# First projections of a two-layer decoder step: where ScalarE loads its sigmoid table, in which order the first block's gates and weight parts are made, and how many result tiles are split beside the last block's gates

## The reference

```python
proj = u @ w_in                            # u = rms_norm(x), w_in 2048 x 5120
xr, gate = proj[..., :D_RNN], proj[..., D_RNN:]          # D_RNN = 2560
xc = conv_b + sum(xpad[:, k:k + T] * conv_w[k] for k in range(4))
xb = xc.reshape(B, T, N_LRU_BLOCKS, LRU_BLOCK)           # 10 blocks of 256
r = sigmoid(einsum('btnc,ncd->btnd', xb, w_r) + b_r)
i = sigmoid(einsum('btnc,ncd->btnd', xb, w_i) + b_i)
log_a = -8 * r * softplus(-lam);  a = exp(log_a)
b = sqrt(-expm1(2 * log_a)) * (i * xc)
h_t = a_t * h_{t-1} + b_t                                # a scan over the tokens
y = (h * silu(gate)) @ w_out                             # w_out 2560 x 2048
```

## Time and profile before

| | |
|---|---|
| median of 3 executions | 1761.04 us (1760.8 to 1763.99) |
| the profiled execution | 1762.91 us, span 1761.2 us |
| PE busy | 1699.5 us (96% of the span), 13907 matmuls |
| DVE busy | 1151.5 us (65%) |
| ACT busy | 973.4 us (55%) |
| POOL busy | 235.6 us (13%) |

### The profile page before, as it was taken

How to read it: one execution, slowest core, us unless ns; L and a number is a source line. 1 busy time by engine, 2 the same in 40 slices (tenths; PEclk the granted TensorE clock), 3 DMA queues, 4 the chain that set the end, 5 groups by cost and what they waited for, 6 DMA issues and landing times.

```text
span 1761.2 us, 34973 instructions
## 1 busy us (share of the span) xinstructions
PE 1699.5 (96%) x13907; PEld 1645.7 (93%) x13907; DVE 1151.5 (65%) x1921; ACT 973.4 (55%) x1643; POOL 235.6 (13%) x182
## 2 busy tenths in 40 slices
PE   7989999999999999999999999999999999899996
PEld 7889999999999999999999999999998999899995
DVE  5878888888889522468767566665666666722365
ACT  6656665566566422355566666666675666522344
POOL 2000000000000010103232222222321111011110
PEclk9999999999999999999999999999999999999998
DMA  8423333233235233664622222222225787423565
GB/s 278 130 85 105 101 109 109 85 113 104 89 113 180 72 93 89 189 178 126 195 85 61 73 73 60 85 60 61 85 61 151 233 249 234 142 84 87 153 179 179
DMA packets 317096, 217.63 MB, mean 124 GB/s; under 512 B 9265, under 2 KB 287937, under 8 KB 316865
## 3 DMA queue, kind: packets, MB, share of 16 engines
q1 hardware_dynamic: 309724, 197.08, 38.1%
q10 hardware_dynamic: 4356, 9.32, 1.4%
q0 software_dynamic: 2864, 9.15, 1.4%
HBM read 195.10 MB, written 20.42 MB: 122 GB/s over the span
## 4 chain that ended last, share of the span: by engine, by line
PE 41%; DVE 5%; issue 2%; ACT 1%; DMA 1%; SPq 1%; ACTq 0%; DVEq 0%
PE PS L858 11%; PE PS L859 10%; PE PS L860 10%; PE Z L1279 2%; DVE T L2638 1%; PE Z L1289 1%; PE Z L1313 1%; PE Z L1185 1%; PE Z L1216 1%; DVE Y L2885 1%; PE Z L1182 1%; PE Z L1194 1%; PE Z L1183 1%; PE Z L1218 1%; PE Z L1217 1%
## 5 line engine op out<-in xcount | busy, mean ns | idle before, releaser
L858 PE MATMUL PS<-U,WS 128*128 128x272 f32 x2528 | 747.0, 295 | 12.9 <-DVE WS L2202 2.7
L860 PE MATMUL PS<-U,WS 128*128 128x272 f32 x2528 | 732.6, 290 | 0.0
L859 PE MATMUL PS<-U,WS 128*128 128x272 f32 x2528 | 730.9, 289 | 0.0
L858 PEld LDWEIGHTS PS<-U,WS 128*128 128x128 f32 x2528 | 478.4, 189 | 19.6 <-issue 9.2
L859 PEld LDWEIGHTS PS<-U,WS 128*128 128x128 f32 x2528 | 478.1, 189 | 2.0
L860 PEld LDWEIGHTS PS<-U,WS 128*128 128x128 f32 x2528 | 477.5, 189 | 0.0
L2177 DVE TENSOR_TENSOR WS<-raw,WS 128x1024 fp32r<-128x1024 f32 (+1 forms) x184 | 231.7, 1260 | 192.3 <-ACT WS L1492 190.8
L1492 ACT ACTIVATE WS<-raw 128x1024 fp32r<-128x1024 f32 (+1 forms) x186 | 192.3, 1034 | 249.5 <-PE PS L860 229.6
L736 POOL TENSOR_TENSOR raw<-raw,GN 128x1024 f32<-128x1024 f32 x76 | 151.0, 1987 | 517.6 <-DMA raw<-in_b_w_in_dram 443.4
L973 PE MATMUL PS<-U,WS 128*128 128x272 f32 x432 | 125.2, 290 | 0.0
L975 PE MATMUL PS<-U,WS 128*128 128x272 f32 x432 | 125.0, 289 | 0.0
(11 more groups left out here) (384 smaller groups left out, 3587.3 us busy)
## 6 DMA issues: line engine op xcount, KB each, us to landing
raw<-in_a_w_in_dram SPq DMA_DIRECT2D x80, 512.0 KB, 3.8
raw<-in_b_w_in_dram SPq DMA_DIRECT2D x64, 512.0 KB, 4.1
raw<-in_a_w_out_dram SPq DMA_DIRECT2D x32, 512.0 KB, 3.9
KPG<-in_cache_k_dram SPq DMA_DIRECT2D x64, 256.0 KB, 3.1
raw<-in_b_w_out_dram SPq DMA_DIRECT2D x32, 512.0 KB, 3.9
VPG<-in_cache_v_dram SPq DMA_DIRECT2D x60, 256.0 KB, 3.3
T<-scratch_x SPq DMA_DIRECT2D x64, 136.0 KB, 3.3
RAW<-in_a_w_out_dram SPq DMA_DIRECT2D x12, 512.0 KB, 4.0
```

The costliest lines, as they stand in the source:

```text
L858: pe.matmul(psum, w_hi, x_hi, start=first, stop=False)
L859: pe.matmul(psum, w_hi, x_lo, start=False, stop=False)
L860: return pe.matmul(psum, w_lo, x_hi, start=False, stop=last)
```

## The change

There is a new one-column tile `WARM`, and `sigmoid_table()` writes a Sigmoid of one column into it, so that the table load stands at that place. It is called in block 0 ahead of the gates, and in every later block in `two_strips(i, 1)` after `keep(p, 2)`. In block 0 the difference 0 and unit 8's high part come earlier, the gate sigmoids come ahead of the two SiLU sigmoids, and DVE follows that order. In block 9 output unit 1's weights and the tiles 8 and 9 are split between the gate sigmoids, the tiles 10 and 11 and output unit 2's weights ahead of `chain_square` (on DVE ahead of `one_minus_a2`, which now precedes the tiles 12 to 15).

```diff
--- before.py
+++ after.py
@@ -206,6 +206,7 @@
+        WARM, _ = sb("WARM", [P, 1])
@@ -1676,6 +1677,9 @@
                     T[:, 4 + 2 * g + o, 0:TOK].rearrange("p (a n) -> p a n", a=2), gate_bank(n, i)[:, :, 0:HALF],
                     ACT.Sigmoid, bias=CH[:, 2 * i + o, ROW_BR + g:ROW_BR + g + 1]).then_inc(gates_out, 1)
 
+            def sigmoid_table():
+                nc.scalar.activation(WARM[:], GN[:, 0, 0:1], ACT.Sigmoid)
+
             def first_block():
                 gate_high(0)
                 conv_tap(0, 0)
@@ -1688,22 +1692,23 @@
                     x_scaled(kt)
                 high(7, 1, 3)
                 conv_high(0, 1)
+                act.wait_ge(unit_done, 7)
+                difference_high(0, U[:, 0:KQ, half(1)])
                 difference_high(1, XT[:, 0, 0])
+                high(8, 0, 4)
                 difference_high(2, XT[:, 2, 0])
                 difference_high(3, XT[:, 1, 0])
-                act.wait_ge(unit_done, 7)
-                difference_high(0, U[:, 0:KQ, half(1)])
-                high(8, 0, 4)
-                sigmoid_gate(0, 0)
+                sigmoid_table()
+                second_half(8)
                 gate_sigmoid(0, 0)
-                second_half(8)
                 gate_sigmoid(0, 1)
-                sigmoid_gate(0, 1)
                 first_sum(8, 0)
                 gate_sigmoid(0, 2)
+                gate_sigmoid(0, 3)
                 second_sum(0)
+                sigmoid_gate(0, 0)
+                sigmoid_gate(0, 1)
                 third_sum(0)
-                gate_sigmoid(0, 3)
 
             def two_strips(i, q, last):
 
@@ -1743,6 +1748,8 @@
                 act.wait_ge(s_done, 3 * p + 2)
                 act.wait_ge(strip_out, 4 * i + 2 * q)
                 keep(p, 2)
+                if q:
+                    sigmoid_table()
                 if last and q:
                     y_back(3)
                 if q == 0:
@@ -1761,16 +1768,19 @@
                 if last:
                     for kt in range(1, 5):
                         y_split(kt)
+                    act.wait_ge(y_done, i * 2)
                     sigmoid_gate(i, 0)
                     y_split(5)
-                    act.wait_ge(y_done, i * 2)
                     gate_sigmoid(i, 0)
                     y_split(6)
                     gate_sigmoid(i, 1)
+                    high(B0 + 1, 1, (B0 + 1) // 2, done=A_UNITS)
                     y_split(7)
                     gate_sigmoid(i, 2)
+                    y_split(8)
                     sigmoid_gate(i, 1)
                     gate_sigmoid(i, 3)
+                    y_split(9)
                     return
                 m, p = pair(i + 1, 0)
                 second_half(m)
@@ -1789,12 +1799,12 @@
             first_block()
             for i in range(1, NBLK):
                 block_a(i, i == NBLK - 1)
-            high(B0 + 1, 1, (B0 + 1) // 2, done=A_UNITS)
-            y_split(8)
-            y_split(9)
             chain_decay(NBLK - 1)
+            y_split(10)
+            y_split(11)
+            high(B0 + 2, 0, (B0 + 2) // 2)
             chain_square(NBLK - 1)
-            for kt in range(2 + UT, KD):
+            for kt in range(12, KD):
                 y_split(kt)
 
             def square(n, par, src):
@@ -1806,7 +1816,7 @@
             def pair_b(i, first):
                 for n in range(6):
 
-                    if not (first and n == 0):
+                    if not (first and n <= 1):
                         tiles = B_TILES[B_FIRST[n + 1][1]] if first and n < 5 else B_TILES[(n + 1) % 3]
                         high(i * 6 + (B0 + n + 1), (n + 1) % 2, i * 3 + (B0 + n + 1) // 2, tiles)
                     if first and n == 1:
@@ -2455,18 +2465,18 @@
                 token_difference(3, XD1[:, 1], XX[:, KQ:UT, half(1)], XX[:, 0:KQ, half(1)])
                 conv_low(0, 0)
                 conv_low(0, 1)
-                difference_low(1, 1, XT[:, 0, 0], XT[:, 0, 1])
-                difference_low(2, 2, XT[:, 2, 0], XT[:, 2, 1])
-                difference_low(3, 3, XT[:, 1, 0], XT[:, 1, 1])
+                difference_low(0, 1, U[:, 0:KQ, half(1)], U[:, KD:KD + KQ, half(1)])
+                difference_low(1, 2, XT[:, 0, 0], XT[:, 0, 1])
                 out_gate(0, 0)
-                difference_low(0, 4, U[:, 0:KQ, half(1)], U[:, KD:KD + KQ, half(1)])
+                out_gate(0, 1)
+                low(8, 0)
+                difference_low(2, 3, XT[:, 2, 0], XT[:, 2, 1])
+                difference_low(3, 4, XT[:, 1, 0], XT[:, 1, 1])
                 weight_sums(8, 0)
-                low(8, 0)
-                out_gate(0, 1)
                 second_weights(8, 0)
-                silu(0, 0)
                 sum_low(0, 2, WSS[:, 0])
                 sum_low(0, 3, WSS[:, 1])
+                silu(0, 0)
 
             def two_strips(i, q, last):
 
@@ -2526,14 +2536,17 @@
             last_block = NBLK - 1
             for i in range(1, NBLK):
                 block_a(i, i == last_block)
+            low(B0 + 1, 1)
             silu(last_block, 1)
-            low(B0 + 1, 1)
             y_rest(8)
             y_rest(9)
             gated_input(last_block)
-            for kt in range(2 + UT, KD):
+            y_rest(10)
+            y_rest(11)
+            low(B0 + 2, 0)
+            one_minus_a2(last_block)
+            for kt in range(12, KD):
                 y_rest(kt)
-            one_minus_a2(last_block)
 
             def out_tile(of, m, n, par):
 
```

## The result

The changed kernel takes 1748.86 us (median of 5 runs, 1747.04 to 1752.01) against 1761.04 us before; ratio 0.993, 95% interval 0.9917 to 0.9943. Forecast were 1750.3 us in a range of 1746.5 to 1755.5. The profiled execution took 1747.57 us (span 1745.8).

The account below looks back on a forecast made before the run. PE, busy 96% of the span, was taken as the bound; 3.45 + 1.1 + 7.3 + 0.4 - 1.5 = 10.75 us off the profiled 1762.91 gave 1752.15, and 1.87 lower for the median, 1750.3 us; range 1746.5 to 1755.5.

Parts of the forecast that it names:

- Block 0's restart: End of block 0: PE starts block 1 at about 89.7 instead of 93.15, 3.45 us gained, with 3.2 us idle before.
- The clock there: Behind block 0's gap: a shorter clock fall, 1.5 us lost instead of 2.6, so 1.1 us gained; bounds 0 and 2.6.
- Blocks 1 to 8: Gate group 2 no longer waits for sigmoid 0 behind the table load: 8 x 0.92 = 7.3 us gained.
- The cover: Blocks 1 to 8: ACT's 3.17 us idle ahead of the convolution's high part takes the load's 1.28 + 0.2 us.
- the margin of 2.7 us: Blocks 1 to 8: DVE finishes the convolution's parts at 190.7, PE reads them from 193.4, 2.7 us later.
- Block 9: After its gates: one 2.4 us gap at tile 12; 0.4 us gained, 1.5 us lost to a clock fall, together -1.1.
- Sum: All terms from block 0 to block 9, with both clock falls: 10.75 us less, median 1750.3 us.
- rival (a): The clock holds behind the gap of block 0, block 9 or both: 1747.3 to 1750.3 us; chance 25%.
- The rival that would have made it slower: Block 0's later weight sums delay unit 10's load, so PE waits in block 1: 1765 us; 3% with other slower causes.

Follow-up runs that it names:

- block 0 alone: The kernel before with only the change's block 0 edits (table ahead of the gates, gate sigmoids first, weight sums later): 1757.59 us, ratio 0.9981.
- blocks 1 to 9 alone: The kernel before with only the sigmoid table loaded in advance in blocks 1 to 9: 1754.24 us, ratio 0.996.
- block 9 alone: The kernel before with only the new order behind block 9's gates on ACT and DVE: 1761.71 us, ratio 1.0.
- three and five loads: The changed kernel with three or five table loads in place of one at each of nine places in blocks 1 to 9: 1750.75 and 1758.79 us.

## Why the prediction was right

- **Block 0's restart.** 3.45 us, as forecast, and by the step named: the weight sum on DVE, then `first_sum` ahead of the last two sigmoids. Moving that one instruction moved the restart by 1.7 us, and 2.3 with PE's gates 0.6 us earlier in that profile. The gap is 2.6 us by the profile where I counted 3.2, since PE's gates ran 0.6 us later against ACT in these executions than in the one that I counted from (in the kernel with block 0 alone it was 3.05). This isn't the change's doing: in two experiments whose block 0 is the old one (blocks 1 to 9 alone, block 9 alone) PE's gates are as late, and the old wait of 1.8 us in block 0 is 1.2 us. Over the twelve profiles they begin 2.0 to 2.2 us behind the pair in three and 2.6 in nine; why stays open.
- **The clock there.** I took a fall of 1.5 us for certain, by a border between 1.76 us and 2.0 us of idleness. This step was wrong as put. Six profiles have this 2.6 us gap: the clock fell in four, held in two; it held behind 3.05 us in a seventh and fell in all three behind 4.6 us. So the term is 2.6 us gained less 1.5 us in part of the runs, not 1.1. It is the prediction's rival (a), and its reading, that one gap can come out either way from run to run, is what the runs show.
- **Blocks 1 to 8.** Forecast 7.3 us, measured 7.4 (0.92 each). The cover held with 1.65 us left, and the runs with three and five loads bear out the margin of 2.7 us behind the idle time: 1.3 us of work beyond the idle time cost nothing, 4.2 us cost 0.59 us per block.
- **Block 9.** Forecast 0.4 us without the clock, measured 0.69; gap 2.07 us against 2.4. ACT and DVE handed over in the order worked out, and taking the two operations from in front of tile 12 took the gap away. The clock fell behind this gap in four of seven profiles.
- **Sum.** By stretches, without any fall after: 3.45 + 2.6 + 7.4 + 0.7 = 14.1 us; with both, 11.2. The three medians of the change are 12.2, 11.0 and 12.6 us below the kernel before, between these. Forecast were 10.75, the sum with both falls, which is why it lies at the slow side. That a forecast with a wrong clock step came within 1.5 us is partly luck: the step decides over 3 us at most, and the 15 executions spread over 5 (1746.8 to 1752.0 us).
- The first profile shows 15.4 us. 2.9 us of it lie in the last column, far behind the change, and 1.9 us the other way ahead of it; a comparison of two spans alone would have put both to the change.
- The rival that would have made it slower (unit 10's load behind the later weight sums) took nothing in the changed kernel. The load was issued at 91.48 us, right where it was worked out (89.65 + 1.89), and landed 3.96 us later; the prediction counted 3.2 us, too little even for the kernel before (3.73), and needed less than 5.2. Its place was rightly seen: as soon as the restart came 2.3 us earlier, unit 10's rest was the next wait.

## What to carry to other kernels

A table load can be moved off a critical sigmoid at no cost by a one-column activation in an idle stretch, if everything between is of the kind that shows no load; the cover is that idle time plus the slack of whoever reads what stands behind it. When a queue is reordered, look for the operation that now stands ahead of the critical one and ask its producer: here one weight sum, whose own engine had been given three more things to do first. And here a gap of two or three microseconds on TensorE had to be priced with a fall of its clock in about every second profile (8 of 15), 1.5 us in most, on top of the idle time.

## What the runs showed of the hardware that had not been expected

The length of one idle stretch of PE doesn't decide alone whether the granted clock falls to 1.2 GHz. Counted over the twelve profiles, between 44 and 612 us: 1.6 us: no fall in twelve gaps; 1.75 to 1.79 us: one in four; 2.07 us: four in seven; 2.26 us (block 9 with five loads): none in one; 2.6 us: four in six; 3.05 us: none in one; 4.6 us: three in three. In two profiles of one and the same program (the changed kernel's first and third) the same two gaps had no fall and two. A fall cost 1.4 to 2.0 us at these places, 0.3 us where a wait behind it vanished in exchange (block 0 alone), and 2.6 us behind 4.6 us of idleness. The Trainium skill ("TensorE: Matmul & The Clock Gate", section "Part 1: The HAM clock gate") says that the monitor runs freely and that one kernel therefore meets it differently from run to run; the counts above agree with it.

A table load and the first activation behind it are 1.28 + 0.2 us in all these rows, and loads in a row take 1.5 us each (178.09, 179.59 and 181.09 us in the kernel with three).
